# New places in SBUF for the split operands of three feed-forward networks

## The reference

```
def swiglu(x, w_gate, w_up, w_down):
    return (jax.nn.silu(x @ w_gate) * (x @ w_up)) @ w_down

first_block:   h = x + 0.5 * rms_norm(swiglu(rms_norm(x), ffn1...))
               h = h + rms_norm(hybrid_mixer(rms_norm(h)))          # attention and dilated attention, gated
               h = h + 0.5 * rms_norm(swiglu(rms_norm(h), ffn2...))
second_block:  x = x + mod * gated_merge(mlstm, diff_attention, ssd)
               x = x + mod * conv_ffn(modulate(rmsnorm(x)))

def conv_ffn(h, w_up, conv_w, w_down):
    a, g = jnp.split(dwconv(h @ w_up, conv_w), 2, axis=-1)
    return (jax.nn.silu(g) * a) @ w_down
```

## The kernel before

| operand | place in `parts`, before: feed-forward 0 / 1 / 2 |
|---|---|
| upper weights `ring_hi` | 0 / 0 / 0 |
| lower weights `ring_lo` | 6160 / 6160 / 6160 |
| lower inputs `u_lo` | 12304 / 12368 / 12368 |
| upper inputs `u_hi` | 14448 / 14448 / 14448 |
| `hidden_hi` | 16496 / 16496 / 16496 |
| `hidden_lo` | 17040 / 17040 / 17104 |

## Time and profile before

### The profile page before, as it was taken

The page is one execution under the profiler, slowest core; times in us unless marked ns, Lnnn a source line. Parts: engine busy times, 40 slices in busy tenths (PEclk is TensorE's granted clock), DMA queues, the critical chain, the costliest instruction groups (busy, mean ns, idle before and its releaser), DMA issues.

```text
span 1260.3 us, 24245 instructions
## 1 busy us (share of the span) xinstructions
PE 1196.8 (95%) x9052; PEld 1117.7 (89%) x9052; DVE 842.0 (67%) x1146; ACT 629.4 (50%) x1008; POOL 545.7 (43%) x283
## 2 busy tenths in 40 slices
PE   6999998998999999999999999997999898999998
PEld 6999998976878999999999888986777797999998
DVE  7788884865873467777654852688746585655555
ACT  5534445526651454554545546466426534655553
POOL 0355556632560542444534644568430374123331
PEclk9999998999999989999989999999999999999999
DMA  8678763433333547888514334223223154555553
GB/s 314 229 277 283 270 226 120 151 115 120 103 102 127 171 170 258 277 288 278 195 34 149 114 106 128 76 99 99 85 83 101 54 183 151 167 186 192 188 186 114
DMA packets 58095, 207.03 MB, mean 164 GB/s; under 512 B 6576, under 2 KB 8240, under 8 KB 57776
## 3 DMA queue, kind: packets, MB, share of 16 engines
q1 hardware_dynamic: 49824, 177.23, 42.2%
q0 software_dynamic: 6912, 25.17, 5.8%
q10 hardware_dynamic: 1296, 3.74, 0.9%
HBM read 205.07 MB, written 1.05 MB: 164 GB/s over the span
## 4 chain that ended last, share of the span: by engine, by line
PE 69%; DVE 13%; issue 6%; ACT 5%; POOL 4%; DMA 3%; DVEq 0%; SPq 0%; POOLq 0%; ACTq 0%
PE psum L620 18%; PE psum L621 18%; PE psum L622 18%; DVE parts L2085 4%; DMA low<-stream 2%; POOL own_parts L2797 2%; PE psum L960 2%; POOL high L2880 2%; PE psum L631 1%; PE psum L632 1%; PE psum L633 1%; PE psum L754 1%; DVE high L2116 1%; PE psum L645 1%; PE psum L908 1%
## 5 line engine op out<-in xcount | busy, mean ns | idle before, releaser
L620 PE MATMUL psum<-parts 128*128 128x256 f32 x1584 | 443.5, 280 | 20.7 <-DVE parts L2085 10.0
L621 PE MATMUL psum<-parts 128*128 128x256 f32 x1584 | 446.5, 282 | 0.0
L622 PE MATMUL psum<-parts 128*128 128x256 f32 x1584 | 442.7, 280 | 0.0
L620 PEld LDWEIGHTS psum<-parts 128*128 128x128 f32 x1584 | 300.7, 190 | 23.8 <-issue 16.2
L2805 POOL TENSOR_TENSOR parts<-low,parts 128x1024 fp32r<-128x1024 f32 x60 | 171.4, 2856 | 336.9 <-ACT parts L1440 336.9
L621 PEld LDWEIGHTS psum<-parts 128*128 128x128 f32 x1584 | 300.8, 190 | 0.0
L622 PEld LDWEIGHTS psum<-parts 128*128 128x128 f32 x1584 | 300.5, 190 | 0.0
L2797 POOL TENSOR_TENSOR own_parts<-low,parts 128x1024 fp32r<-128x1024 f32 x76 | 187.8, 2484 | 196.7 <-ACT parts L1509 196.4
L1440 ACT ACTIVATE parts<-low 128x1024 fp32r<-128x1024 f32 x198 | 205.2, 1054 | 122.5 <-DMA low<-stream 118.1
L2085 DVE TENSOR_TENSOR parts<-low,parts 128x1024 fp32r<-128x1024 f32 x138 | 181.1, 1346 | 20.9 <-ACT parts L1440 20.1
L622 PE MATMUL psum<-scratch_parts,own_parts 128*128 128x256 f32 (+1 forms) x496 | 150.9, 304 | 0.0
(11 more groups left out here) (355 smaller groups left out, 2166.6 us busy)
## 6 DMA issues: line engine op xcount, KB each, us to landing
low<-stream SPq DMA_DIRECT2D x334, 512.0 KB, 3.5
high<-conditioning POOLq DMA_DIRECT2D x48, 512.0 KB, 5.5
high<-wuq ACTq DMA_DIRECT2D x1, 1152.0 KB, 11.1
low<-x SPq DMA_DIRECT2D x4, 256.0 KB, 5.9
high<-ctx ACTq DMA_DIRECT2D x1, 1024.0 KB, 6.2
out<-low SPq DMA_DIRECT2D x8, 128.0 KB, 1.8
low<-cst ACTq DMA_DIRECT2D x1, 850.5 KB, 4.7
low<-vec ACTq DMA_DIRECT2D x1, 157.5 KB, 5.8
```

The lines of the kernel that those rows point to most:

```text
L620: pe.matmul(out, w_hi[:, cols_], x_hi, start=start, stop=False, **kw)
L621: pe.matmul(out, w_hi[:, cols_], x_lo, start=False, stop=False, **kw)
L622: return pe.matmul(out, w_lo[:, cols_], x_hi, start=False, stop=stop, **kw)
```

## The change

The places of the six operands are no longer a table of starts with shifts. A function lays them out in a given order, each at the next place with a given remainder modulo 128. Each feed-forward has its own order:

| operand | place in `parts`, after: feed-forward 0 / 1 / 2 | modulo 128, before | modulo 128, after |
|---|---|---|---|
| `ring_hi` | 0 / 0 / 0 | 0 / 0 / 0 | 0 / 0 / 0 |
| `ring_lo` | 8720 / 6144 / 8816 | 16 / 16 / 16 | 16 / 0 / 112 |
| `u_lo` | 6144 / 14448 / 6240 | 16 / 80 / 80 | 0 / 112 / 96 |
| `u_hi` | 14960 / 12400 / 14960 | 112 / 112 / 112 | 112 / 112 / 112 |
| `hidden_hi` | 17008 / 16496 / 17008 | 112 / 112 / 112 | 112 / 112 / 112 |
| `hidden_lo` | 8192 / 17008 / 8288 | 16 / 16 / 80 | 0 / 112 / 96 |

The end of `parts` moves from 17616 to 17520, and with it `cond_sums` and the first of the places for conditioning tiles, by 96 elements. No instruction, wait, transfer or order is added, removed or moved; the three products read the same values.

```
-PARTS, END_PARTS = regions([("ring_hi", RING * TILE), ("ring_lo", RING * TILE), ("u_lo", DC * T), ("u_hi", DC * T),
-                            ("hidden_hi", 2 * T), ("hidden_lo", 2 * T), ("shifts", 208)], 0)
-PART_STARTS = ({"ring_lo": 16, "u_hi": 112, "u_lo": 16, "hidden_hi": 112, "hidden_lo": 144},
-               {"ring_lo": 16, "u_hi": 112, "u_lo": 80, "hidden_hi": 112, "hidden_lo": 144},
-               {"ring_lo": 16, "u_hi": 112, "u_lo": 80, "hidden_hi": 112, "hidden_lo": 208})
+PART_WIDTHS = {"ring_hi": RING * TILE, "ring_lo": RING * TILE, "u_hi": DC * T, "u_lo": DC * T,
+               "hidden_hi": 2 * T, "hidden_lo": 2 * T}
+LINES = 128
+def part_starts(order):
+    starts, at = {}, 0
+    for name, place in order:
+        at += (place - at) % LINES
+        starts[name] = at
+        at += PART_WIDTHS[name]
+    return starts, at
+PART_STARTS = [part_starts(order) for order in (
+    (("ring_hi", 0), ("u_lo", 0), ("hidden_lo", 0), ("ring_lo", 16), ("u_hi", 112), ("hidden_hi", 112)),
+    (("ring_hi", 0), ("ring_lo", 0), ("u_hi", 112), ("u_lo", 112), ("hidden_hi", 112), ("hidden_lo", 112)),
+    (("ring_hi", 0), ("u_lo", 96), ("hidden_lo", 96), ("ring_lo", 112), ("u_hi", 112), ("hidden_hi", 112)),)]
+END_PARTS = max(end for _, end in PART_STARTS)
...
-        ring_lo = ffn_parts("ring_lo", RING, TILE)
-        u_hi, u_lo = ffn_parts("u_hi", DC, T), ffn_parts("u_lo", DC, T)
-        hidden_hi, hidden_lo = ffn_parts("hidden_hi", 2, T), ffn_parts("hidden_lo", 2, T)
+        ring_hi, ring_lo = ffn_parts("ring_hi", RING)[0], ffn_parts("ring_lo", RING)
+        u_hi, u_lo = ffn_parts("u_hi", DC), ffn_parts("u_lo", DC)
+        hidden_hi, hidden_lo = ffn_parts("hidden_hi", 2), ffn_parts("hidden_lo", 2)
```

More of the change, by code:

```diff
@@ L395, in two_blocks, with ffn_parts @@
         p2_lo_ctx = u_parts[:, :].rearrange("p (c t) -> p c t", c=DC)
[L397 to L402, removed]
-        ring_lo = ffn_parts("ring_lo", RING, TILE)
-        u_hi, u_lo = ffn_parts("u_hi", DC, T), ffn_parts("u_lo", DC, T)
-        hidden_hi, hidden_lo = ffn_parts("hidden_hi", 2, T), ffn_parts("hidden_lo", 2, T)
+        def ffn_parts(name, n):
+            return [parts[:, starts[name]:starts[name] + PART_WIDTHS[name]].rearrange("p (a b) -> p a b", a=n)
+                    for starts, _ in PART_STARTS]
+        ring_hi, ring_lo = ffn_parts("ring_hi", RING)[0], ffn_parts("ring_lo", RING)
+        u_hi, u_lo = ffn_parts("u_hi", DC), ffn_parts("u_lo", DC)
+        hidden_hi, hidden_lo = ffn_parts("hidden_hi", 2), ffn_parts("hidden_lo", 2)
         inv_mix = view(MEM, "root")
```

## The result

The changed kernel is slower: median 1269.95 us over 14 runs against 1263.12 us for the kernel before over 14 runs, ratio 1.0051 (95% interval 1.0030 to 1.0073). I had forecast 1259.5. The single runs scatter by several us in both kernels (1263.5 to 1276.6 and 1259.5 to 1271.2), so I read the cause from the pace of the triples, which hardly scatters. The changed kernel's lines are 12 further on: L632, L633, L634 are L620, L621, L622 of before, L2097 is L2085.

The account below looks back on a forecast made before the run. TensorE's pace was taken to bound feed-forwards 1 and 2, and mostly VectorE feed-forward 0. From the median, 1262.91 - 3.4 = 1259.5 us (3.2 from the second gap, 0.2 from feed-forward 0); range 1256.0 to 1267.0.

Parts of the forecast that it names:

- Step 1: Second gap (L621 to L622) in feed-forwards 1 and 2: falls from 0.118 to 0.115, 3.2 us gained.
- a price for each pair: Pair reading: a gap is long when weights being loaded and inputs being streamed share a remainder; chance 0.38, 1259.5 us.
- Step 2: First and third gaps of the triple: taken as unchanged; if all three gaps came to 0.1135, 6.5 us gained.
- the sign that the prediction had named for step 2: In the profile after, a first or third gap that grew by what the second lost would show it wrong.
- The remainders modulo 32: Operand places taken modulo 32, so all layouts fall into remainders of 0 and 16; no row tested a shift of 32.
- mixed rival: Feed-forward 1 gains 1.6 to 3.3 us, feed-forward 2 takes the pace of `out2`, losing 1.7; 1262.2 us, chance 0.20.
- The slower rival: Feed-forwards 1 and 2 both run at 0.350 or above, 3.5 to 7.5 us lost; 1266.6 us, chance 0.22.
- Step 3: Feed-forward 0: same gain per triple, mostly hidden by VectorE; TensorE's 14.1% chain share gives 0.2 us gained.
- Steps 4 to 6: Writers of moved places, 0.1 us either way; `cond_sums` and conditioning place moved by 96, nothing; nothing else moves.
- step 4: Writers of the moved places: nothing in feed-forwards 1 and 2, 0.1 us either way in feed-forward 0.

Follow-up runs that it names:

- the all-alike layouts: Kernel before with both weights at remainder 0 and both inputs at one distance behind them, six distances; paces 350.3 to 359.6 ns a triple.

## Why the prediction was wrong

**What bounds the kernel.** Right: in the two profiles TensorE's pace in feed-forwards 1 and 2 turned into time (3.4 and 5.8 us by the pace, 3.1 and 6.4 by the length of the stages), and places of operands set that pace. The pace gives 9.2 us for the two. The ratio of all runs gives 6.4 us, with 3.8 to 9.2 as its interval, so it agrees with the pace only at its upper end; the two profiles differ by 11.2. Part of that lies in the scatter of single executions: the profiled one after is 3.3 us above its median, the one before 1.1 below.

**Step 1, the second gap.** This is the step that failed. I took the second gap to be long because lower weights and lower inputs lie at one remainder, and put it at 115 once they don't. With them 16 apart it measured 118.1, 117.5 and 119.2. Feed-forward 0 shows it cleanest, for there only the lower inputs had moved. The assumption beneath it was a price for each pair. The layouts with other lower weights and the all-alike layouts contradict it: what a gap takes depends on all the distances together.

**Step 2, the other two gaps.** I took them as unchanged, and they carried nearly all of the loss: the first rose by 6.0, 4.9 and 4.4 ns, the third by 3.1, 2.4 and 5.8, while the second changed by -0.2, -0.8 and 0.9. It was the sign that the prediction had named for step 2, except that the second gap had lost next to nothing.

**The remainders modulo 32** were a choice that no row tested, as the prediction said. The period is 64. Modulo 64 the layouts after are (16, 48, 0), (0, 48, 48) and (48, 48, 32), none of which any stage of the kernel before has; `out2` has (16, 16, 0). So the mixed rival was wrong too: it gave feed-forward 2 the 350 of `out2`, and it measured 357.7. Feed-forward 1, where it saw a gain, lost 6.5.

**The slower rival** is what happened: both feed-forwards above 0.3491, 1266.6 to 1270.6 forecast for it, 1269.95 measured. That the time lies inside is in part luck, for feed-forward 2 ran at 357.7, past the 353.8 that the rival had as its slowest. Its argument, that each other layout in the kernel was slower than the present one, was the better reading of the earlier trace rows. I gave it 0.22, and the range ended at 1267.0, only 0.4 us into its 1266.6 to 1270.6. Of about 40 layouts tried since, none is faster than the present one, and only two others are within 1 ns of it (lower inputs at 15, and (16, 111, 15)).

**The rule of the Trainium skill** in "SBUF — State Buffer" would have made the sum nothing, as the prediction read it: TensorE has one read port for the moving operand and an independent one for weight loads (section "Who interferes with whom"), and it never waits on anyone (section "SBUF: two separate sides"). The runs speak against that conclusion: 346.7 to 362.6 ns for the same three matmuls, by places alone. Whether the two ports wait for each other, or something else does it, no run shows.

**Step 3, feed-forward 0.** In kind right, as far as the counts tell: 329 triples in 120 us before and after, while its undisturbed triples were 8.9 ns longer. In size not settled. I put 14% of the full effect on the clock; here that is 0.7 us, and alone its layout gave a ratio of 1.0027 with an interval from 0.3 to 6.6 us. The stage's length scatters, 191.5 to 195.4 us in five profiles with the old layout, and it doesn't follow the pace: with 350.3 ns a triple it was 190.9 us long (in the kernel with the layouts of other stages).

**Steps 4 to 6** fit: VectorE's, ScalarE's and GpSimd's busy times moved by 3.2 us at most, and with the old remainders and the moved `cond_sums` the ratio is 1.0005 (0.9982 to 1.0028). A part under 0.3% would not be seen there, and the writers at the new places (step 4) were not measured alone.

## What to carry to other kernels

When TensorE is the bound, with matmuls like these (`fp32r`, 128x256, a weight load each) at the full clock, compare the start-to-start pace of equal matmuls in different stages: a difference there was here a matter of placement, and a stage with a good pace is a pattern to copy whole. What is copied is the set of distances between all operands of the loop modulo 64 elements; no change of a single operand's place made it faster here, and one element can undo it. A table of measured layouts beats a rule for a single pair, so try several layouts in one kernel, one per repeated stage, and read the pace from the trace.

## What the runs showed of the hardware that I had not expected

- The pace of matmuls of 128x256 with a 128x128 load each depends on the distances of their operands modulo 64 elements (256 bytes), from 115.6 ns a matmul (346.7 / 3) to 120.9 (362.6 / 3), repeats to 0.1 ns, and did not change with everything moved by 8 elements, with another tensor or another order of the regions.
- A single element of shift changes a triple by up to 13.3 ns (lower inputs 16 to 17).
- It shows only at the full clock (2.4 GHz). Feed-forwards 1 and 2 begin at half clock (1.2 GHz), and there a triple takes 0.640 us, each matmul 0.213, in the traces of all these kernels, whatever the layout. First the row of 1074.4 to 1079.9 us after (the last three columns are the granted clock, 0.50, the DMA share and GB/s), then the timeline of PE in it, five triples in 3.20 us:

```profile
1074.40:1079.90 5.50, 5.50 (x26) 5.50 (x27) 5.17 (x13) 4.13 (x7) 0.00 (x0) 0.50 0.01 3
```

```profile
1075.08 0.41 PE L632 MATMUL psum<-parts 128*128 128x256 f32 x1
...
1078.28 0.41 PE L632 MATMUL psum<-parts 128*128 128x256 f32 x1
```

- Uneven gaps inside a triple don't tell which operand is badly placed: a layout with a second gap of 115.0 had the first and third at 121.4 and 123.5. What inside the chip makes the pace, and whether a layout below 346.7 exists, stays open; no experiment separated the weight loads from the streamed inputs.
